# Low weight halves kept in the ring's slots, eight high halves, and a new order of work at the norms of a fused two-block transformer kernel

## What is computed

```python
def squared_relu_mlp(x, w_up, w_down):          # w_up 1024 x 4096, w_down 4096 x 1024
    return jnp.square(jax.nn.relu(x @ w_up)) @ w_down

def first_block(x, ...):
    h = x
    for layer in range(2):
        mix = diff_attention(h, ...) if layer == 0 else moba_attention(h, ...)
        h = layer_norm(DEEPNORM_ALPHA * h + mix, ln1_g[layer], ln1_b[layer])
        h = layer_norm(DEEPNORM_ALPHA * h + squared_relu_mlp(h, w_up[layer], w_down[layer]),
                       ln2_g[layer], ln2_b[layer])
    return h

def second_block(x, c, ...):
    u = modulate(rmsnorm(h, norm1), sh1, sc1)
    h = h + g1 * token_mixer(u, w_in, w_ret_o, w_uq, w_ukv, w_mla_o, w_out, ...)
    u = modulate(rmsnorm(h, norm2), sh2, sc2)
    h = h + g2 * hier_moe(u, w_grp, b_grp, w_exp, b_exp, w1, w3, w2)
    return rmsnorm(h, final_norm)
```

## Time and profile before

| | |
|---|---|
| Median of three runs | 1192.47 us (1191.81 to 1195.05) |
| Profiled execution | 1190.7 us, span of its profile 1188.9 us |
| Busy share of the span | TensorE 94%, VectorE (DVE) 59%, ScalarE (ACT) 47%, GpSimd (POOL) 4% |
| Granted TensorE clock, mean | 0.974 of full speed |
| Transfers | 285.17 MB, mean 240 GB/s |

### The profile page before, as it was taken

How to read it: one execution, slowest core, us unless ns; L and a number is a source line. 1 busy time by engine, 2 the same in 40 slices (tenths; PEclk the granted TensorE clock), 3 DMA queues, 4 the chain that set the end, 5 groups by cost and what they waited for, 6 DMA issues and landing times. The chain is left out here.

```text
span 1188.9 us, 17973 instructions
## 1 busy us (share of the span) xinstructions
PE 1118.6 (94%) x7231; PEld 898.8 (76%) x7231; DVE 699.5 (59%) x1041; ACT 556.3 (47%) x953; POOL 52.4 (4%) x94
## 2 busy tenths in 40 slices
PE   7998899999999999999998999999999999889676
PEld 5987688888789987888887878988887866546333
DVE  3487867778766667778778626745456643312112
ACT  4567556556545646555655424345543322213112
POOL 5000000010000000010000000000000000000000
PEclk9999999999999999999998999999999989979988
DMA  9943378888755333888873652455647799999995
GB/s 273 290 168 104 107 224 295 292 280 292 244 163 191 108 117 130 321 293 275 285 262 100 137 177 72 142 206 180 209 139 262 280 374 369 389 398 386 417 416 225
DMA packets 126510, 285.17 MB, mean 240 GB/s; under 512 B 12222, under 2 KB 72891, under 8 KB 118369
## 3 DMA queue, kind: packets, MB, share of 16 engines
q1 hardware_dynamic: 116512, 249.29, 59.9%
q0 software_dynamic: 9920, 34.80, 9.1%
HBM read 281.87 MB, written 2.20 MB: 239 GB/s over the span
## 5 line engine op out<-in xcount | busy, mean ns | idle before, releaser
L2000 DVE TENSOR_TENSOR w_lo<-ring,w_hi 128x1024 fp32r<-128x1024 f32 (+1 forms) x272 | 320.3, 1212 | 101.1 <-ACT w_hi L1507 91.7
L1507 ACT ACTIVATE w_hi<-ring 128x1024 fp32r<-128x1024 f32 (+1 forms) x272 | 277.0, 1047 | 102.8 <-PE acc L680 77.2
L678 PE MATMUL acc<-w_hi,x_two 128*128 128x512 f32 (+2 forms) x320 | 128.5, 402 | 5.3 <-DVE x_two L1985 4.1
L680 PE MATMUL acc<-w_hi,x_two 128*128 128x512 f32 (+2 forms) x320 | 123.4, 386 | 0.0
L679 PE MATMUL acc<-w_lo,x_two 128*128 128x512 f32 (+2 forms) x320 | 123.3, 385 | 0.0
L678 PE MATMUL pp<-x_two,w_hi 128*128 128x256 f32 x384 | 112.5, 293 | 0.0
L679 PE MATMUL pp<-x_two,w_hi 128*128 128x256 f32 x384 | 108.5, 283 | 0.0
L680 PE MATMUL pp<-x_two,w_lo 128*128 128x256 f32 x384 | 108.5, 283 | 0.0
L678 PE MATMUL acc<-w_hi,hid_hi 128*128 128x512 f32 x256 | 99.8, 390 | 0.0
L680 PE MATMUL acc<-w_hi,hid_lo 128*128 128x512 f32 x256 | 99.6, 389 | 0.0
L679 PE MATMUL acc<-w_lo,hid_hi 128*128 128x512 f32 x256 | 99.6, 389 | 0.0
(11 more groups left out here) (397 smaller groups left out, 2135.4 us busy)
## 6 DMA issues: line engine op xcount, KB each, us to landing
ring<-in_w_up_dram SPq DMA_DIRECT2D x32, 1024.0 KB, 5.7
ring<-in_w_down_dram SPq DMA_DIRECT2D x32, 1024.0 KB, 6.6
exp_ring<-in_w_dram SPq DMA_DIRECT2D x32, 1024.0 KB, 11.3
stage<-in_w_ada_dram POOLq DMA_DIRECT2D x48, 512.0 KB, 6.2
ring<-in_w_in_dram SPq DMA_DIRECT2D x24, 1024.0 KB, 5.3
ring<-in_w_in_a_dram SPq DMA_DIRECT2D x12, 1024.0 KB, 14.2
mod<-in_w_dram SPq DMA_DIRECT2D x19, 512.0 KB, 12.9
ring<-in_w_kv_shared_dram SPq DMA_DIRECT2D x8, 1024.0 KB, 6.2
```

Of the source, the lines that this page charges most:

```text
L678: pe.matmul(out, lhs[0], rhs[0], start=start, stop=False)
L680: return pe.matmul(out, lhs[1], rhs[0], start=False, stop=stop)
L1507: act.activation(shaped(high_half(b, k), raw), raw, ACT.Copy).then_inc(S["hi_ready"], 1)
L2000: dve.tensor_tensor(shaped(low_half(b, k), raw), raw, shaped(high_half(b, k), raw), ALU.subtract).then_inc(S["lo_ready"], 1)
```

## The change

Six edits go together:
- For blocks 12 to 99 (`in_place`) DVE writes the low half over the raw data in the ring (`ring_lo` is the same memory as `ring`). The slot is then free when TensorE has used the block, so SP waits for `half_used` there instead of `lo_ready`.
- `w_lo` goes; `w_hi` has eight slots. The high halves of most of the in-place blocks use all eight; elsewhere the high halves use four and the low ones the other four.
- At norms 0 and 2 tile 0 is normalised first and split while tile 1 is summed; TensorE does `up(0)` and `up(1)` by token tile (`up_tile`: 256 wide with the high weights, 128 wide with the low ones), each with tile 0 first. ACT and DVE split the blocks b + 1 and b + 2 inside the norm.
- `tile_first_out` does tile 0 of two blocks before tile 1 of either. It is used at norms 1 and 3.
- The last two pairs of an MLP are ordered so that tile 0 of the last stands ahead of tile 1's last parts of the one before.
- In the last quad of experts five constant products stand between the first and the third weights' products.

```diff
-HIGHS = 4
+HIGHS = 8
-LOWS = 4
...
+def in_place(b):
+
+    return B_ATT[0] + 12 <= b < B_RQK
...
+def high_slot(b, k):
+
+    return half_index(b, k) % (HIGHS if in_place(b) else HIGHS // 2)
+
+
+def high_depth(x):
+
+    return HIGHS if half_index(B_ATT[0] + 14, 0) <= x < half_index(B_UQ + 3, 0) else HIGHS // 2
...
+        with nc.sbuf_tensor("ring_lo", [128, RING, 2048], f32r) as ring_lo:
+            low_ring = ring_lo
-        w_lo = sb("w_lo", [128, LOWS, HALF], f32r)
...
-            return tp if v % 2 else pp
+            if v == 0:
+                return acc[:, 0:2, :]
+            return pp if v % 2 else tp
...
-            return w_lo[:, half_index(b, k) % LOWS, :]
+            if in_place(b):
+                return raw_half(b, k, low_ring)
+            return w_hi[:, HIGHS // 2 + high_slot(b, k), :]
...
-                    if is_split(old):
+                    if in_place(old):
+                        sp.wait_ge(S["half_used"], half_index(old, 1) + 1)
+                    elif is_split(old):
...
-                for j in range(4):
-                    if j % 2 == 0:
-                        half_ready(b, j // 2)
-                    part(0, j, 0)
-                    if j == 1:
+                for i in range(2):
+                    for j in range(4):
+                        if j % 2 == 0:
+                            half_ready(b + i, j // 2)
+                        part(i, j, 0)
+                    if i == 0:
                         turn()
                 pe.wait_ge(S["x_split"], base + 3)
-                for j in range(4):
-                    last = part(0, j, 1)
-                    if j % 2 == 1:
-                        last.then_inc(S["half_used"], 1)
-                for i in range(1, 4):
+                for i in range(2):
+                    for j in range(4):
+                        last = part(i, j, 1)
+                        if j % 2 == 1:
+                            last.then_inc(S["half_used"], 1)
+                for i in range(2, 4):
...
+                def up_tile(v, c, k, q):
+
+                    tok = slice(q * 128, (q + 1) * 128)
+                    sums = up_banks(v)[:, c, :].rearrange("p (a n) -> p a n", a=2)[:, :, tok]
+                    if k == 0 and q == 0:
+                        half_ready(b + v, c)
+                    for kt in range(4 * k, 4 * k + 4):
+                        hi, lo = w_parts(b + v, c, slice(128 * kt, 128 * kt + 128))
+                        if kt:
+                            pe.matmul(sums[:, 0, :], lo, x_hi[:, kt, tok], start=False, stop=False)
+                        last = pe.matmul(sums, hi, x_two[:, :, kt, tok], start=(kt == 0), stop=(kt == KT - 1))
+                        if kt == 0:
+                            pe.matmul(sums[:, 0, :], lo, x_hi[:, kt, tok], start=False, stop=False)
+                    if k == 1 and q == 1:
+                        last.then_inc(S["half_used"], 1)
...
+                norm_tile(2 * layer, 0)
+                busy(2)
+                for k in range(2):
+                    pe.wait_ge(S["x_split"], base + 1 + k)
+                    for c in range(2):
+                        up_tile(0, c, k, 0)
+                norm_tile(2 * layer, 1)
+                for c in range(2):
+                    for k in range(2):
+                        up_tile(1, c, k, 0)
+                for k in range(2):
+                    pe.wait_ge(S["x_split"], base + 3 + k)
+                    for c in range(2):
+                        up_tile(0, c, k, 1)
+                for c in range(2):
+                    for k in range(2):
+                        up_tile(1, c, k, 1)
+                down(0)
+                for v in range(1, PAIRS - 2):
                     up(v + 1)
-                    if v == 0:
-                        pe.wait_ge(S["ln_stat"], 4 * layer + 2)
                     down(v)
-                pe.wait_ge(S["hid_ready"], PAIRS * (layer + 1))
-                for f in range(2):
-                    half_ready(b + 31, f)
-                for q in range(QT):
-                    for half in range(2):
+                up(PAIRS - 1)
...
+                for v in range(PAIRS - 2, PAIRS):
+                    pe.wait_ge(S["hid_ready"], PAIRS * layer + v + 1)
+                    for f in range(2):
+                        half_ready(b + min(2 * v + 2, 31), f)
+                    last_parts(v, 0, (0, 1))
+                    if v == PAIRS - 2:
+                        last_parts(v, 1, (0,))
+                last_parts(PAIRS - 2, 1, (1,))
+                last_parts(PAIRS - 1, 1, (0, 1))
...
+                    if s + 1 == QUADS:
+                        busy(5, turn_bank)
...
+                b = (B_MLP[0], B_ATT[1], B_MLP[1])[i]
                 norm_root(i, 0)
-                if i == 1:
-                    scaled(0, 1)
-                    norm_root(i, 1)
-                    high(B_ATT[1] + 1)
-                    scaled(0, 1)
-                    return
-                scaled(0)
+                scaled(0, 1)
+                high_part(b + 1, 0)
                 norm_root(i, 1)
-                scaled(1)
+                high_part(b + 1, 1)
                 scaled(0, 1)
-                high((B_MLP[0], B_ATT[1], B_MLP[1])[i] + 1)
+                if i != 1:
+                    high(b + 2)
...
+                normalise(0)
+                sum_part(i, b, 1, 0)
+                half_sum(i, b, 1, 1)
+                split_input(1)
+                link(half_stats(1, 1))
+                tile_stat(1)
+                split_input(1)
+                normalise(1)
+                low((B_MLP[0], B_ATT[1], B_MLP[1])[i] + 1)
+                split_input(2)
                 if i != 1:
-                    sum_part(i, b, 1, 0)
-                    normalise(0)
-                else:
-                    normalise(0)
-                    sum_part(i, b, 1, 0)
-                link(sum_part(i, b, 1, 1))
-                tile_stat(1)
-                if i == 1:
-                    split_input(1)
-                normalise(1)
+                    low((B_MLP[0], B_ATT[1], B_MLP[1])[i] + 2)
```

More of the change, by code:

```diff
@@ L689, in w_parts @@
             def w_parts(b, k, cols):
-                return high_half(b, k)[:, cols], low_half(b, k)[:, cols]
+                low = low_half(b, k)
+                if len(low.shape) == 3:
+                    assert cols.stop - cols.start == 128
+                    return high_half(b, k)[:, cols], low[:, cols.start // 128, :]
+                return high_half(b, k)[:, cols], low[:, cols]
             def arrive(b):
@@ L965, in norm_tile @@
             def norm_tile(i, q):
-                busy(0 if i == 1 else 2)
                 pe.wait_ge(S["ln_out"], QT * i + q + 1)
@@ L1003, in down @@
                             last.then_inc(S["half_used"], 1)
-                up(0)
-                for v in range(PAIRS - 1):
+                norm_tile(2 * layer, 0)
[8 more added lines that the diff above has]
+                        up_tile(1, c, k, 0)
@@ L1010, in mlp, with last_parts @@
                     down(v)
-                pe.wait_ge(S["hid_ready"], PAIRS * (layer + 1))
-                for f in range(2):
-                    half_ready(b + 31, f)
-                for q in range(QT):
-                    for half in range(2):
+                up(PAIRS - 1)
+                def last_parts(v, q, halves):
+                    for half in halves:
                         for f in range(2):
-                            last = down_part(PAIRS - 1, 2 * f + half, q)
+                            last = down_part(v, 2 * f + half, q)
@@ L1035, in _ @@
                 attention(layer)
-                for q in range(QT):
-                    norm_tile(2 * layer, q)
-                busy(2)
                 mlp(layer)
@@ L1666, in mlp @@
                     h = relu[:, v % 2, :]
-                    used(b + max(2 * v - 1, 0))
+                    used(b + (v if v < 2 else 2 * v - 1))
                     if j >= 2:
@@ L1671, in mlp @@
                         .then_inc(S["rest_ready"], 1)
-                    high(b + 2 * v + 2 - (v > 0) if v < PAIRS - 1 else b + 31)
+                    if v:
+                        high(b + 2 * v + 1)
                     act.wait_ge(S["sum_done"], j + 1)
@@ L1996, in low_part @@
                 dve.wait_ge(S["hi_ready"], x + 1)
-                if x >= LOWS:
-                    dve.wait_ge(S["half_used"], x - LOWS + 1)
+                if x >= HIGHS // 2 and not in_place(b):
+                    dve.wait_ge(S["half_used"], x - HIGHS // 2 + 1)
                 raw = raw_half(b, k)
```

38 lines of the change are left out of this document (18 added, 20 removed).

## The result

Over 22 runs of each kernel on the same chips the changed kernel takes 1193.10 us in the median (1189.74 to 1200.58) and the kernel before 1188.01 us (1181.80 to 1195.05; the three runs shown ahead of the prediction lay in its upper part). The ratio is 1.0049, 95% interval 1.0033 to 1.0065: slower by 0.49%, which is 5.8 us of 1188 (the two medians stand 5.1 us apart). The forecast was 6.1 us more than before. In absolute time it was 1198.6 us, 5.5 too much, because the three runs it started from were slower ones; 1193.10 lies just inside the lower end of its range, 1193.0 to 1203.0.

A forecast was written before the change was run, and what follows sets the result against it. TensorE, busy 94% of the span, was taken as the bound. Terms 2.4 - 0.2 + 6.8 - 2.9 = +6.1 us on the 1192.47 us median gave 1198.6 us, own range 1196 to 1201.5, range with rivals 1193.0 to 1203.0.

The forecast's parts named there:

- Slot rule, steady state: Blocks 12 to 99: giving ring slots back after TensorE's use costs nothing, with some 3 to 4 us of cover.
- Norms 0 and 2: Attention to MLP: `down(0)` starts 1.2 us later at each, +2.4 us together, from -1.8 to +3.2.
- rival 3: Norms 0 and 2: narrow products run at their width, 2.4 becomes -1.8; +1.9, 1194.4 us; chance 0.08.
- The sign named for this: Norms 0 and 2: 128-wide products start 0.105 to 0.12 us after the one before; wrong if 0.06 apart.
- Norm 1: Last MLP products and the norm: about 1 us wait at pair 15, first split 0.8 sooner; net -0.2 us.
- Norm 3: Block 96 on: later turn, 4.6 us wait, block 98 ends +2.9 us; late block 105 makes it +6.8 at `w_uq`.
- rival 2: Clock falls in two new idle stretches, before block 97 and the latent copies: 2.9 to 5.8 us more; chance 0.13.
- Rival 1: SP queue behind norm 3: block 105 lands early enough, only the 2.9 us of reordering counts; +2.2, 1194.7 us; chance 0.14.
- Rival 4: Expert stage: its transfer waits absorb the delay, only the end counts; -2.9, 1189.6 us; chance 0.10.
- The last quad: Last experts: five constant products fill the gap and keep the clock up for the third products; -2.9 us, upper bound 0.

The follow-up runs named there:

- r1_ring: The kernel before with the new slot rule alone (blocks 12 to 99, eight high halves, SP waiting for the use): ratio to before 1.0051.
- g2_norm1: The kernel before with the last-quad fillers and the change's order at norm 1, nothing else: ratio to before 0.9958.
- g1_order: The changed kernel with block 105's split moved behind the latent copies on ACT and behind the second rotation on DVE: ratio to before 1.0018.
- b2_fwd: The changed kernel with only blocks 12 to 97 in place and ACT's and DVE's work on block 97 moved ahead at norm 3: ratio to before 0.9988.
- e1_turn3: The changed kernel with norm 3's old order, one block's tile 0 ahead of tile 1: ratio to before 1.0064.
- f2_before_fill: The kernel before with the five constant products in the last quad and nothing else: ratio to before 0.9975.
- e4_nofill: The changed kernel without the five constant products in the last quad: ratio to before 1.0076.
- e2_ringc: The changed kernel with blocks 96 to 99 no longer in place, norm 3's reorder kept: ratio to before 1.0071.
- b1_two: The changed kernel with norm 3's old order and only blocks 12 to 97 in place: ratio to before 1.0008.
- g3_fwd_order: The changed kernel with blocks 12 to 97 in place, block 97's splits moved ahead at norm 3, block 105's split behind the latent copies: ratio to before 0.9956.

## Why the prediction was right, point by point

**Direction and size.** +6.1 us forecast, +5.8 measured. The sum is better than its terms, and that is luck: norm 3 was put 3.2 us too low, norm 1's gain 1.2 us too low, and the stretches of the trace add up to more than the medians show (below). What was right without luck is the direction, and that the loss is at norm 3 and in the queue behind it.

**Slot rule, steady state: 0.** Right, by r1_ring's first five columns. That is as far as it goes: the rule's cost stands where the stream of blocks leaves the steady state, at the `w_uq` blocks.

**Norms 0 and 2: +1.2 each.** +1.1 each, in every kernel with that code. The first split came 5.0 us after the last attention product, and the pair of narrow products takes 0.23 us, as chosen. So rival 3 (products at their width, 0.18 a pair) is out. Only the sum of the pair was right, though: it was made of two equal distances of 0.115, and the rows have 0.17 and 0.06. The sign named for this, a distance of 0.105 to 0.12 ahead of each narrow product, did not come, and the 0.06 that was to prove it wrong stands behind each of them; the sign was badly chosen, since a product's start tells of its neighbour too. The edit at norms 0 and 2 was never undone alone; its price is read from the stretches. The Trainium skill's figure (TensorE: Matmul & The Clock Gate, Back-to-back issue gap; 81 ns per 128-wide product) would make a pair 0.196 with 0.115 for the wider one, and the rows at 142.24 and 142.47 show more; the measurement decides.

**Norm 1: -0.2, bounds -1.0 and +1.0.** Outside its bounds: the MLP takes 1.5 more and the stretch behind it 2.9 less, -1.4 in all. The wait at pair 15 was as described, about 1 us. TensorE's waits in the changed kernel:

```profile
318.59 0.50 PE L701 MATMUL acc<-w_hi,hid_hi 128*128 128x512 f32 x1 [1.08 <-DVE hid_lo L2324]
...
329.15 0.50 PE L701 MATMUL acc<-w_hi,x_two 128*128 128x512 f32 x1 [0.92 <-DVE x_two L2044]
```

and in the kernel before, at the same norm:

```profile
327.17 0.50 PE L678 MATMUL acc<-w_hi,x_two 128*128 128x512 f32 x1 [1.65 <-DVE x_two L1985]
...
332.10 0.50 PE L678 MATMUL acc<-w_hi,x_two 128*128 128x512 f32 x1 [1.01 <-DVE x_two L1985]
```

The mistake was in the norm. Of two waits for a split one is left, 0.92 us; the prediction gave tile 0 of block 49 the role of cover for the later turn and didn't count that it also fills the wait for tile 1's split. g2_norm1 has the norm's order without the reorder of the last pairs and gains 1.5, so that reorder is about neutral here. In MLP 1, for which the sum has no such term, it costs the same 1.5, of which "to 96" gives back about 1 (8.9 to 10.4 us instead of 10.3 to 11.6).

**Norm 3: +2.9 at block 98, +6.8 at `w_uq`.** The mechanism was right in each step: the turn 0.96 us later, the wait of 4.61 us (4.6 forecast), block 102 released by block 98's use, block 105 not yet landed when ACT should copy latents (ACT waited 8.31 us for it, rows at 684.33). The sizes: +5.4 from 96 to 100 and +4.6 from there, 10.0 in all. The 2.5 us too little on the way to 100 are the clock, by the 18 products that took 5.44 us instead of 3.3: the prediction's rival 2 said that 4 us of idle time may do this to the products behind, and put 0.13 on it. It was no rival but a part of the same event. In g1_order the same wait, 4.60 us, was followed by a clock of 0.50 from 650 to 653 and 0.93 from 653 to 656, and the stretch took 22.72, so this part varies from run to run; b2_fwd, where the wait is gone, takes 17.45. The second idle stretch that rival 2 named, ahead of the latents' transposes, came too (4.79 us, to 687.25), and the first `w_uq` products behind it ran at 0.50. But they had done so in the kernel before, with 1.10 us idle just ahead of them: from the first of them, the next 60 took 14.6 us before and 14.7 after. So it added nothing there. In the queue the prediction had the steps right and their pace too fast: block 105 was issued 11.6 us after 102, not 10.7, and 102 itself 2.7 us later than forecast, most of it by the clock. The step to g1_order shows that the second part is block 105 ahead of the latent copies, as the prediction had it.

**Rival 1, the queue doesn't pass it on:** out, by r1_ring. **Rival 4, the expert stage absorbs it:** the stretches sum to about 11 us at `w_uq` (1.1 - 1.4 + 1.1 + 0.3 + 10.0), less about 3 for the fillers is 8; 5.8 were measured, interval 3.9 to 7.7. Full absorption is excluded, a part of 2 us is not. Nor is it needed: with g1_order's 31.6 us at norm 3 in place of the changed kernel's 34.5 the sum is 5 instead of 8. e1_turn3, where less was measured than the trace promises, points the other way. What the expert stage does with a delay stays open to 2 or 3 us.

**The last quad: -2.9.** f2_before_fill gives 0.9975, 3.0 us (0.2 to 5.7); the rows at 1171.83 show the third products at full clock, and the 64 of them take 3.6 us to the next work instead of 6.3 before. e4_nofill fits, 1.0076 against 1.0049, with intervals that overlap. The gain depends on the gap: in r1_ring, without fillers, it was 2.67 us long, and the products behind it began at full clock but did not keep it.

```profile
1169.52 0.40 PE L1387 MATMUL pp<-q_t,k_t 128*32 128x256 f32 x1 [2.67 <-DMA w_rest<-in_w_dram]
```

The windows behind it, columns as in the earlier trace rows:

```profile
1170.00:1171.00 1.00, 1.00 (x20) 0.62 (x16) 0.00 (x0) 0.00 (x0) 0.00 (x0) 0.70 1.02 406
1171.00:1172.00 1.00, 1.00 (x16) 0.48 (x12) 0.00 (x0) 0.00 (x0) 0.00 (x0) 0.50 1.01 393
```

Their 64 took 5.3 us there, and the same in e4_nofill, whose gap was also 2.67 us: 1.7 too many, against 2.7 behind the gap of 4.93. The first product behind a gap doesn't tell; the window does.

## What to carry to other kernels

When a buffer is given back later than before, price the last places of the stream and not the steady state: there the wait moves whatever stands behind it in the queue. When a transfer becomes late, look at what stands behind its consumer on the same engine; moving that work ahead of it gave back about 4 us here. Taking blocks out of the ring, so that the transfer starts sooner, paid for it at the end of the MLP (e2_ringc) or left `w_uq` late all the same (b1_two). A shared helper that takes a second block ahead must be followed on every engine at every call: at norms 0 to 2 the splits moved with it, at norm 3 they did not.

## What the runs showed of the hardware

- Idle TensorE time of 4.61 us was followed by products at the lower clock (0.50 from 654 to 657, changed kernel), and so was 4.93 us before the change. After 2.67 us (r1_ring) the first products ran at full clock and then at 0.50 from 1171 to 1173. What it cost was about 2.1 us behind 4.61, 2.7 behind 4.93 and 1.7 behind 2.67.
- The length of the last gap alone does not decide: 1.45 us before block 96's tile 1 was followed by 1.00 (before), and 1.10 us before the first `w_uq` product by 0.50 in the kernel before and by 1.00 in f2_before_fill, with the same code there. Behind five fillers a gap of 1.23 us was followed by full clock (f2_before_fill, 64 products in 3.6 us).
- Two loads of 128-byte pieces (`w_uq`; L430, L451 or L453) held SP for 1.9 to 6.2 us. For block 102's two it was 4.3 to 6.2 where the last one-megabyte load had been issued 1.1 us ahead (b1_two, g3_fwd_order, b2_fwd), 3.0 at 2.3 us (before), and 1.9 to 2.8 at 4.6 us (r1_ring, changed, g1_order).
- A pair of one 256-wide and one 128-wide fp32r product, each with its own weight load, takes 0.23 us (142.24 to 142.47); by width alone, at the 0.12 us that a 256-wide one takes in a row of its kind, it would be 0.18.
